# Delta rule levels taken in two steps each, and projection units and transpose groups re-placed in the forgetting attention

## The reference, cut to what matters

```python
# gated delta rule, a head: chunks of tokens
L = where(strict, (k * beta) @ k.T * decay, 0)
sol = triangular_solve(eye + L, rhs)          # the inverse of a unit lower triangle
v_new = u - w @ state                         # chunk after chunk
o = q_dec @ state + a_qk @ v_new
state = state * g_last + k_dec.T @ v_new
o = rms_norm(o, norm_g) * silu(z)

# forgetting attention, a block of 128 queries
logits = q @ k.T + c[t] - c[s]                # masked to keys at or before the query
o = softmax(logits) @ v * silu(z)
```

## Time and profile before

| | |
|---|---|
| median of 3 runs | 1862.23 us (1860.49 to 1862.98) |
| the profiled execution | 1862.04 us |
| its span, first to last instruction | 1860.3 us |
| Delta phase | from about 25 to 722 us of the span |
| one Delta iteration | 78.9 us (402.78 to 481.69) |
| attention phase | from about 1134 to 1626 us |
| one attention pair | 58.5 us (1290.59 to 1349.12) |
| mean granted TensorE clock | 0.981 |

### The profile page before, as it was taken

The page is one execution under the profiler, slowest core; times in us unless marked ns, Lnnn a source line. Parts: engine busy times, 40 slices in busy tenths (PEclk is TensorE's granted clock), DMA queues, the critical chain, the costliest instruction groups (busy, mean ns, idle before and its releaser), DMA issues. The chain is left out here.

```text
span 1860.3 us, 29061 instructions
## 1 busy us (share of the span) xinstructions
PE 1733.1 (93%) x11293; PEld 1305.4 (70%) x11293; DVE 917.7 (49%) x1736; ACT 754.6 (41%) x1232; POOL 265.9 (14%) x211
## 2 busy tenths in 40 slices
PE   7999999999999987979989998999999999899798
PEld 5777777777777765858877887565665555588687
DVE  3767676675766725653331200344444443575523
ACT  3436354463545532142222311555545555440411
POOL 2212122221221151200000001111111110012000
PEclk9999999999999988989989999999999999999899
DMA  5121010211201121131130202111111101051311
GB/s 136 41 55 35 24 47 13 51 33 33 35 24 35 58 92 57 34 122 56 38 104 19 72 2 47 36 41 30 42 32 41 41 18 43 1 170 35 111 45 48
DMA packets 113079, 92.86 MB, mean 50 GB/s; under 512 B 19696, under 2 KB 95664, under 8 KB 112944
## 3 DMA queue, kind: packets, MB, share of 16 engines
q1 hardware_dynamic: 112944, 91.02, 17.1%
HBM read 82.51 MB, written 8.49 MB: 49 GB/s over the span
## 5 line engine op out<-in xcount | busy, mean ns | idle before, releaser
L481 PE MATMUL gdn_unit<-part_hi,gdn_w_hi 128*128 128x512 f32 x512 | 235.4, 460 | 0.2 <-DVE gdn_w_lo L831 0.2
L483 PE MATMUL gdn_unit<-part_hi,gdn_w_lo 128*128 128x512 f32 x512 | 201.8, 394 | 0.0
L482 PE MATMUL gdn_unit<-part_lo,gdn_w_hi 128*128 128x512 f32 x512 | 200.6, 392 | 0.0
L2053 DVE CUSTOM_DVE_ANT_0 fa_probs<-fa_scores,fa_decay 128x896 f32<-128x896 f32 (+7 forms) x128 | 97.0, 758 | 123.1 <-PE fa_scores L1870 77.7
L1822 PE MATMUL fa_unit<-part_hi,fa_w_hi 128*128 128x512 f32 x256 | 115.4, 451 | 17.2 <-ACT fa_qk L1969 15.8
L874 DVE SCALAR_TENSOR_TENSOR x<-gdn_raw,gdn_taps,x 128x512 f32<-128x512 f32 x144 | 123.7, 859 | 5.1
L2002 ACT ACTIVATE fa_probs_t<-fa_turned 128x512 f32<-128x512 f32 (+1 forms) x96 | 52.3, 545 | 158.5 <-PE fa_turned L1887 158.1
L446 POOL TENSOR_TENSOR gdn_w_lo<-ring,gdn_w_hi 128x1024 fp32r<-128x1024 f32 x31 | 75.1, 2423 | 268.2 <-ACT gdn_w_hi L675 268.2
L483 PEld LDWEIGHTS gdn_unit<-part_hi,gdn_w_lo 128*128 128x128 f32 x512 | 96.1, 188 | 21.5
L1996 ACT ACTIVATE fa_probs<-fa_probs,fa_top 128x896 f32<-128x896 f32 (+7 forms) x128 | 99.6, 778 | 22.1 <-DVE fa_top L2053 18.1
L481 PEld LDWEIGHTS gdn_unit<-part_hi,gdn_w_hi 128*128 128x128 f32 x512 | 96.9, 189 | 15.0 <-issue 3.6
(11 more groups left out here) (304 smaller groups left out, 3642.7 us busy)
## 6 DMA issues: line engine op xcount, KB each, us to landing
ring<-in_gdn_w_in_dram SPq DMA_DIRECT2D x32, 512.0 KB, 4.1
ring<-in_ple_w_gate_dram SPq DMA_DIRECT2D x32, 256.0 KB, 3.0
ring<-in_fox_w_in_dram SPq DMA_DIRECT2D x32, 256.0 KB, 2.9
ring<-in_fox_w_in_dram SPq DMA_DIRECT2D x16, 512.0 KB, 4.8
fa_decay<-c_rows_scratch SPq DMA_DIRECT2D x64, 128.0 KB, 3.0
in_x_tile<-in_x_dram SPq DMA_DIRECT2D x8, 512.0 KB, 6.0
gdn_g_bc<-g_rows_scratch SPq DMA_DIRECT2D x8, 512.0 KB, 8.7
x_scratch<-x SPq DMA_DIRECT2D x8, 512.0 KB, 2.9
```

The lines of the kernel that those rows point to most:

```text
L481: pe.matmul(out, w_hi[:, j % 2, k, :], xh[:, k, ts], start=(k == 0), stop=False)
L482: pe.matmul(out, w_hi[:, j % 2, k, :], xl[:, k, ts], start=False, stop=False)
L483: mm = pe.matmul(out, w_lo[:, j % 2, k, :], xh[:, k, ts], start=False, stop=(k == KT - 1))
```

## The change

In the Delta phase a level takes two steps: the transpose of the inverse moves from a step of its own to the front of the next level's step 0 (on ACT its copy too). The chunks start at step 23 instead of 29. The copy of the first half of o moves from 41 to 35, its squares from 53 to 47, its sums from 59 to 53, its norm from 62 to 57. The sums of the keys (45), the norm of the keys (49), the decays (55) and the rest stay.

In the attention phase the fill behind the scores of row 0 has four steps, and none follows at e = 7, so that units end in front of the scores of rows 2, 4 and 7. ACT takes the exponential of head 1 before the last filler point of a row. The two groups of row e = 5 change places, by 1 first.

```diff
-AT_CHUNKS = 29
-AT_O_TAKE = 41
+AT_CHUNKS = AT_LEVELS + 2 * LEVELS
+AT_O_TAKE = 35
-AT_O_SQUARES = 53
+AT_O_SQUARES = 47
-AT_O_SUMS = 59
+AT_O_SUMS = 53
-AT_O_NORM = 62
+AT_O_NORM = 57
...
-                level, what = (s - AT_LEVELS) // 3, (s - AT_LEVELS) % 3
+                level, what = (s - AT_LEVELS) // 2, (s - AT_LEVELS) % 2
...
                             pe.wait_ge(x_made, LEVELS * p + level)
+                            if level == 1:
+                                pe.wait_ge(kd_made, p + 1)
+                            turn(w0, inv_t, t_turned, range(NT // 2))
...
-                    if what == 2 and not last:
-                        pe.wait_ge(x_made, LEVELS * p + level + 1)
-                        if level == 0:
-                            pe.wait_ge(kd_made, p + 1)
-                        turn(w0, inv_t, t_turned, range(NT // 2))
...
-                    if 0 <= level < LEVELS - 1 and what == 2:
-                        act.wait_ge(t_turned, (LEVELS - 1) * p + level + 1)
+                    if 0 < level < LEVELS and what == 0:
+                        act.wait_ge(t_turned, (LEVELS - 1) * p + level)
...
+        def turn_order(e):
+            return (1, 0) if e == 5 else (0, 1)
+
         def pieces_done(n):
             p, e, head = n // (2 * NT), n % (2 * NT) // 2, n % 2
-            return 2 * sides_before(p, e) + (2 * head + 2 if len(sides(e)) == 2 else head + 1)
+            return 2 * sides_before(p, e) + (2 * head + 2 if len(sides(e)) == 2 else turn_order(e).index(head) + 1)
...
                     if e == 0:
-                        fill(3)
+                        fill(4)
                         continue
...
                     for side in sides(e - 1):
-                        for by in range(2):
+                        for by in turn_order(e - 1):
                             if p >= 0:
                                 turn(p, e - 1, side, by)
-                            if e < NT - 1 or by == 0:
+                            if e < NT - 1:
                                 fill(1)
...
                 for e in range(NT):
                     if e == 0:
-                        fill(3)
-                    for side in (sides(e - 1) if e else ()):
+                        fill(4)
+                        if p >= 0:
+                            exponent(p, e, 0)
+                            exponent(p, e, 1)
+                        continue
+                    for side in sides(e - 1):
                         if p >= 0:
                             take_turned(p, e - 1, side)
-                        fill(1)
+                        if e < NT - 1:
+                            fill(1)
                         if p >= 0 and side == 0:
                             exponent(p, e, 0)
+                        if p >= 0 and side == sides(e - 1)[-1]:
+                            exponent(p, e, 1)
                         if e < NT - 1:
                             fill(1)
-                    if p >= 0:
-                        if e == 0:
-                            exponent(p, e, 0)
-                        exponent(p, e, 1)
```

More of the change, by code:

```diff
@@ L796, in _ @@
                                  bv_made, n == NT - 1)
-                    level, what = (s - AT_LEVELS) // 3, (s - AT_LEVELS) % 3
-                    if 0 <= level < LEVELS - 1 and what == 2:
-                        act.wait_ge(t_turned, (LEVELS - 1) * p + level + 1)
+                    level, what = (s - AT_LEVELS) // 2, (s - AT_LEVELS) % 2
+                    if 0 < level < LEVELS and what == 0:
+                        act.wait_ge(t_turned, (LEVELS - 1) * p + level)
                         step(act.activation(inv[:], w0[:, 0:HALF], ACT.Copy), t_copied)
-                        if level == LEVELS - 2:
+                        if level == LEVELS - 1:
                             act.wait_ge(x_made, LEVELS * p + LEVELS - 1)
@@ L1999, in take_turned @@
             def take_turned(p, e, side):
-                act.wait_ge(flipped, 2 * sides_before(p, e) + 2 * side + 1)
+                act.wait_ge(flipped, 2 * sides_before(p, e) + 2 * side + turn_order(e).index(0) + 1)
                 to, source = turned_to(e, side, 0)
@@ L2057, in take_turned @@
             def take_turned(p, e, side):
-                dve.wait_ge(flipped, 2 * sides_before(p, e) + 2 * side + 2)
+                dve.wait_ge(flipped, 2 * sides_before(p, e) + 2 * side + turn_order(e).index(1) + 1)
                 to, source = turned_to(e, side, 1)
```

## The result

The kernel after takes 1852.42 us, the median of 6 runs (1849.38 to 1855.76); the kernel before, on the same chip, 1862.61 us (6 runs, 1860.49 to 1864.68). The ratio is 0.9944, 95% interval 0.9934 to 0.9954: faster by 10.2 us. The forecast was 1847.5 us, with a range from 1834 to 1859. The profiled execution of the kernel after is one of 1850.70 us, span 1849.0. The lines of the kernel after in the attention stand two to five further down (L1822 is L1824, L1887 is L1889, L2075 is L2080), those of VectorE in the Delta phase two further up (L910 is L908, L951 is L949); the product into the inverse, L617, is L621, the chunks' L631 and L637 are L629 and L635.

The account below looks back on a forecast made before the run. PE, busy for 93% of the span, was taken as the bound, so only its waits and its stream's own cost count. From 1862.04 us, attention -22 and Delta phase +7.5 gave 1847.5 us, range 1834 to 1859.

Parts of the forecast that it names:

- Units and row 0's filler: Attention: three unit waits vanish in pairs 1 to 7, 2.6 us a pair; the fourth filler gains 0.5 a pair.
- Row 5's groups: Attention: a group and a filler fill PE's wait for DVE's gate, gaining 1.0 us a pair; 0.35 lost later.
- Merged step: Delta phase: saved re-entry of 0.17 us and tile-shape change of 0.18 cancel; 0 for 35 levels, bounds -6 and +1.
- Sums of o: Delta phase, step 53: PE waits 2.5 us, as ACT has the keys' root before o's copy; +17.4 us in seven iterations.
- L637 and L631: Delta phase, steps 51 and 35: PE's wait for DVE's rest goes, -8.2 us; its wait for the state shrinks, -2.3.
- DVE at steps 47 to 57: Delta phase: POOL's operations in a row cost 0.4 us an iteration more wait at the 2x2 inverses, +2.8.
- Iteration 8: Last Delta iteration: more spread work after o's sums, with root and DVE's last passes beside it; -2.2 us, bounds -5 and 0.
- A: Delta phase: the wait at step 53 is absent or under 0.5 us, so its 17.4 go; 1830 us, chance 0.13.
- B: Attention: waits come back elsewhere, ACT's copy late behind an exponential; half the gain left, -11, 1858.5 us, chance 0.10.
- C: Delta phase, steps 49 to 57: DVE falls behind POOL, PE waits at step 8; slower, 1864 us, chance 0.05.

Follow-up runs that it names:

- units_only: The kernel before with the attention's fourth filler, units in front of the scores and ACT's new order, but row 5's groups in the old order; 1847.62 us.
- turn_only: The kernel before with only the two transpose groups of row 5 in the other order; 1859.06 us.
- merge_only: The kernel before with a level's transpose put in front of the next level's y, levels from step 17, chunks and o's steps unmoved; 1867.43 us.
- swap: The kernel after with the keys' sums at step 47 instead of 45 and o's squares at 46 instead of 47; 1837.08 us.
- sums57: The kernel after with o's sums at step 57 instead of 53 and o's norm at 61 instead of 57; 1862.3 us.

## Why the prediction was right and where it was off

The time is 4.9 us above the forecast (1852.4 for 1847.5), within its own likeliest bounds (1840 to 1855). The mechanism that it put against the change, the wait at the sums of o, is the one that was there, by the steps and almost at the size that it gave. Point by point:

- **Units and row 0's filler.** Forecast 2.6 + 0.5 a pair, less 0.7 for row 7's exponentials: 2.4. `units_only` has 2.40. The unit waits went from 24 to 4, as forecast. (3 x 0.9 is 2.7, not 2.6; it changes nothing.)
- **Row 5's groups.** Forecast 1.0 less 0.35: 0.65 a pair. `turn_only` has 0.74. Pair 55.4 us forecast, 55.35 measured; attention -22 forecast, -22.2 measured. The two costs taken off were not as forecast, so that the sums agree is in part luck: the wait of L1889 for ACT's L1998 is 0.2 to 0.3 us in each of the seven pairs, not 0.7, and L1872's for DVE came 3 times, not in every pair.
- **Merged step.** Forecast 0 (bounds -6 and +1). `merge_only`: -0.8 in seven iterations. Right in size. That the saved re-entry and the change of tile shape are what cancels was argued; no run takes them apart.
- **Sums of o.** Forecast 2.5 x 7 = 17.4; measured 16.1 in seven iterations (2.3 each; 16.4 with the eighth's 0.3), by the very chain of the walk. `swap`, which puts o ahead of the keys, ends it, and the times of ACT's list in both traces show that its order held o: the cause is shown.
- **L637 and L631.** Forecast -8.2 - 2.3 = -10.5. In their place stands one wait of 0.4 us an iteration (2.7 idle for 11.8), -9.1 and the knock-on of the waits that went: right in sum. It is the rest of step 39 (L949) that is waited for, as the walk had it.
- **DVE at steps 47 to 57.** Forecast +2.8 at the inverses, measured +0.5 (8.2 for 7.7). The number was small for a reason that the prediction had not seen: it took this term and the wait at the sums for two costs to be added. They are one lateness; `sums57` shows the hidden part, 16.8 us. Nor does it count POOL's L466, which is in that wait in every kernel.
- **Iteration 8.** Forecast -2.2 (bounds -5 and 0), measured -3.5. `merge_only` and `sums57` show its two sides: where the levels start (5.3 us) and where o's norm ends (6.6 us).
- **What the prediction left out.** It put two things at nothing without a word. One is the clock: in its Delta phase "only waits and interruptions count", and a wait was priced without the stretch of low clock that can follow it, about 1.4 us net for two of them here. The other is all that lies outside the two phases, 3.0 us in the profiled execution.

The miss of 4.9 us is then made up so: 3.0 outside the phases; 1.7 in iterations 1 to 7 (+11.4 for a forecast of 17.4 - 8.2 - 2.3 + 2.8 = +9.7), most of it the low clock; -1.3 in iteration 8 and -0.2 in the attention; and 1.7 between the profiled execution (1850.70) and the median. For the last the runs give a hint only: the three slower executions (1854.1 to 1855.8 us) have a mean granted clock of 0.972 to 0.974, the three faster ones (1849.4 to 1850.8) 0.975 to 0.976. The iteration of 79.9 us that the prediction names does not follow from its own sum: +9.7 in seven gives 80.3, since 79.9 spreads the -2.2 of iteration 8 over the others too. The measured mean is 80.4.

Of the rivals, A (no wait at the sums) was wrong for the change; `swap` makes its condition true and takes 1837.1 us for its 1830, 7 above; 5.8 us of wait came back at the inverses. B is out (pair 55.35). C did not happen in this kernel, but its mechanism is real: `sums57` has it, with 17.3 us more at step 8 than the kernel before, 2.5 an iteration. That its time, 1862.3 us, is near the 1864 of C is chance: C counted the wait at the sums as well, and `sums57` has none there.

## What to carry to other kernels

Before a wait is priced or taken away, ask who else is late at that moment: a wait of the critical engine gives every other engine the same time, and what it covers shows up when it goes and they stay late (16.4 us went, 16.8 came). To gain, take away what makes them late (`swap`: 16.4 went, 5.8 came). Work that needs nothing recent should leave the queue behind a shared resource, and must be kept clear of every other operation that locks it: the same eight operations gained about 7 us in one set of steps and lost about 15 in another. And where one edit of several carries a loss, run the parts alone: here half of the change was worth twice the whole, and two constants in an order list (`swap`) another 15 us.

## What the runs showed of the hardware that was not expected

- A wait of PE of 2.0 to 4.0 us inside a stream that is otherwise 94% busy can be followed by about 3.4 us at a granted clock of 0.5. In the kernel after such an iteration lasted 82.2 us for 80.5, and the next one was 1.0 us shorter. With recurring waits up to 1.7 us it never did, and in one kernel not with 2.0 either.
- A pass, a product or an exponential of DVE whose inputs all lie in SBUF and that starts while GpSimd's operation runs ends 0.14 to 0.56 us behind GpSimd's end whatever its own size: 2.33 us for one of 0.35 (the earlier trace rows have 1.63 for one of 0.49). In the Delta phases of the twelve kernels this is so for all such starts that stand by themselves in the timelines, over 400 of them. Operations that read PSUM (the copy of v_new, the rest, the state) and the clearing of the state ran through at their own length in the same places, 0.29, 0.35, 0.35 and 0.17 us, and so did the statistics of the layer norm behind the phase (0.69 us, six times), though they read SBUF.
- Between two GpSimd operations in a row DVE got in one pass, and three in a row made two passes last 5.51 us together, for 1.5 undisturbed.
- Putting the transposes of a level right in front of its row-turned products, and not behind a filler of their own, changed next to nothing: 35 merged steps, -0.8 us.
